# Second rotation buffers, a fourth score bank, a third bank for the up-projections, and two blocks of x scaled by ScalarE, in a hybrid encoder layer

## The reference, cut to what matters

```python
def hybrid_layer(x, mem, g_pre, w_in, w_conv, attn_sink, g_mem, w_mem_kv, w_up_a, w_up_b, w_up_m, w_out, g_post):
    h = rms_norm(x, g_pre)                       # x: 1024 tokens x 1024
    (a_b, a_c, a_x, a_z, b_q, b_k, b_v, b_z, m_q, m_z, gate_logits) = jnp.split(h @ w_in, idx, axis=-1)
    ya = short_gated_conv(a_b, a_c, a_x, w_conv) * silu(a_z)
    q, k = partial_rope(b_q, pos), partial_rope(b_k, pos)      # 8 query heads, 2 key heads, 64 wide
    yb = window_attention_with_sink(q, k, b_v, attn_sink) * silu(b_z)   # +-128 tokens
    mk, mv = split(rms_norm(mem, g_mem) @ w_mem_kv)            # 256 memory tokens
    ym = memory_cross_attention(m_q, mk, mv) * silu(m_z)
    gates = sigmoid(gate_logits)                               # 3 branches x 1024
    merged = gates[0] * (ya @ w_up_a) + gates[1] * (yb @ w_up_b) + gates[2] * (ym @ w_up_m)
    return x + rms_norm(merged @ w_out, g_post)
```

## Time and profile before

| | us |
|---|---|
| median of 3 runs | 968.27 |
| the three runs | 965.97 to 968.99 |
| the profiled execution | 967.6 |
| its span | 965.8 |

### The profile page before, as it was taken

One profiled execution on the slowest core, in us unless ns is written; L12 is line 12 of the kernel. 1 busy time (PEld: TensorE's weight loads), 2 busy tenths in 40 slices (PEclk: granted clock), 3 DMA queues, 4 the chain that ended last, 5 costly groups with the idle time before them and its releaser, 6 DMA issues. The chain is left out here.

```text
span 965.8 us, 12506 instructions
## 1 busy us (share of the span) xinstructions
PE 925.0 (96%) x4360; PEld 770.9 (80%) x4360; DVE 621.4 (64%) x1055; ACT 419.9 (43%) x800; POOL 386.9 (40%) x266
## 2 busy tenths in 40 slices
PE   5999779999999999999999999999998999999997
PEld 4787668888888888888888888888887788888885
DVE  5799856556565656655568178878896366664443
ACT  7322446444444456544461533333443534332211
POOL 2557834444333344443333844444442635210000
PEclk9999899999999999999999999999999899999999
DMA  7125545243424243434345512323222964542222
GB/s 278 66 75 137 137 134 166 99 145 106 148 99 145 99 134 98 163 104 149 105 141 160 157 55 77 87 85 90 87 68 80 319 227 148 200 169 68 88 88 87
DMA packets 79629, 122.33 MB, mean 127 GB/s; under 512 B 6992, under 2 KB 38864, under 8 KB 79568
## 3 DMA queue, kind: packets, MB, share of 16 engines
q1 hardware_dynamic: 79568, 121.55, 38.7%
HBM read 88.49 MB, written 33.03 MB: 126 GB/s over the span
## 5 line engine op out<-in xcount | busy, mean ns | idle before, releaser
L623 POOL TENSOR_TENSOR ring<-spots,ring 128x512 fp32r<-128x512 f32 x218 | 309.3, 1422 | 406.4 <-ACT ring L1020 394.2
L698 PE MATMUL pm<-hc,ring 128*128 128x512 f32 x728 | 287.9, 395 | 5.7 <-ACT ring L1020 5.5
L700 PE MATMUL pm<-hc,ring 128*128 128x512 f32 x728 | 284.5, 391 | 0.0
L699 PE MATMUL pm<-hc,ring 128*128 128x512 f32 x728 | 284.3, 391 | 0.0
L1020 ACT ACTIVATE ring<-spots 128x512 fp32r<-128x512 f32 x218 | 136.2, 628 | 258.9 <-PE pm L700 191.0
L698 PEld LDWEIGHTS pm<-hc,ring 128*128 128x128 f32 x728 | 137.3, 189 | 33.1 <-issue 6.5
L700 PEld LDWEIGHTS pm<-hc,ring 128*128 128x128 f32 x728 | 137.2, 188 | 29.4
L699 PEld LDWEIGHTS pm<-hc,ring 128*128 128x128 f32 x728 | 137.4, 189 | 26.8
L970 PE MATMUL pm<-hc,ring 128*128 128x512 f32 x192 | 76.1, 396 | 3.3 <-DVE area L1773 3.3
L971 PE MATMUL pm<-hc,ring 128*128 128x512 f32 x192 | 75.8, 395 | 0.0
L972 PE MATMUL pm<-hc,ring 128*128 128x512 f32 x192 | 75.7, 394 | 0.0
(11 more groups left out here) (198 smaller groups left out, 1518.2 us busy)
## 6 DMA issues: line engine op xcount, KB each, us to landing
spots<-in_w SPq DMA_DIRECT2D x116, 256.0 KB, 3.2
raw_d<-area SPq DMA_DIRECT2D x72, 256.0 KB, 2.0
area<-raw_d SPq DMA_DIRECT2D x24, 512.0 KB, 3.5
area<-in_x SPq DMA_DIRECT2D x16, 512.0 KB, 4.9
spots<-in_wup SPq DMA_DIRECT2D x24, 256.0 KB, 3.8
q_d<-area_r SPq DMA_DIRECT2D x16, 256.0 KB, 4.0
area_r<-q_d SPq DMA_DIRECT2D x8, 512.0 KB, 4.3
area<-raw_d SPq DMA_DIRECT2D x16, 256.0 KB, 3.6
```

The lines of the kernel that those rows point to most:

```text
L623: nc.gpsimd.tensor_tensor(ring[:, n % RING, 1, :], operand(n), ring[:, n % RING, 0, :].bitcast(F32), ALU.subtract).then_inc(lo_made, 1)
L698: pe.matmul(bank, hi, moving_hi(k), start=(k == 0), stop=False)
L699: pe.matmul(bank, hi, moving_lo(k), start=False, stop=False)
L700: mm = pe.matmul(bank, lo, moving_hi(k), start=False, stop=(k == HC - 1))
```

## The change

Four parts, and the order of the programs around them:

- **Blocks 6 and 7 of x** are scaled by ScalarE, after its root for them and VectorE's inverse. Product 5 of the first pair has no turns ahead of it, product 6 those of chunk 8, product 7 those of chunks 9 and 10, and from there it is as before.
- **Rotations** have two high buffers and two low ones (the low part overwrites the rotated tile). rope_high waits for no store; times_cos(j) waits for the stores of rotation j - 2. The rotations stand later in the order of each engine, between combinations, weight sums and weight splits; SyncE's stores stand behind more weight loads.
- **Scores**: the fourth head's scores go to pv and wait for the last output to have left it, no longer for the first mask.
- **Up-projections** rotate over three pairs of banks, and three of them run their first three chunks before the fourth. The first gate has the other gate buffer and is loaded at P4 of the last pair, once the last cross scores are done.

The diff, cut to what the prediction speaks of (left out: the same edits of names in the loads, the gate's drain and the semaphores' declarations):

```diff
@@ -89,7 +89,7 @@
 
 AREA = 14400
 X0, B11F, B21F, B12F, B22F, T3F = 0, 8192, 10240, 12288, 0, 2048
-COS0, SIN0, SWAP0, ROT1, QHI0, QLO0, ROT0, VR0, VP0 = 4096, 5120, 6144, 7168, 0, 1024, 2048, 3072, 12288
+COS0, SIN0, SWAP0, ROT1, QHI0, ROT0, VR0, VP0 = 4096, 5120, 6144, 7168, 0, 2048, 3072, 12288
 QS0, KWH0, KWL0, PR0, PTH0, PTL0, OS0, OO0 = 0, 1024, 1792, 2560, 4096, 5632, 7168, 7680
 O0 = 10240
 SIG0, SB0 = 8192, 9728
...
-        rope_hi_f32, rope_lo_f32 = rope_hi_r.bitcast(F32), rope_lo_r.bitcast(F32)
+        rope_high_at = [f32r(QHI0 + n * SEQ, SEQ) for n in range(2)]
+        rope_low_at = [f32r(at, SEQ) for at in (ROT1, ROT0)]
         memx = f32(MX0, 2 * D).rearrange("p (b d) -> p b d", b=2)
...
             return tile_banks[t % 3]
...
 
...
             return f32(Y0 + n % 4 * SEQ, SEQ)
+
+        def score_bank(h):
+            return pv[:, 0:WIN] if h == GROUP - 1 else sa[:, BANKS[h], 0:WIN]
+
+        def gate_of(g):
+            return gate[:, (g + 1) % 2, :]
 
         def bank_of(p, name):
...
+        inv_made, xs_act = sem("inv_made"), sem("xs_act")
...
+        def wait_stored(eng, j):
+            eng.wait_ge(rope_stored[j], 16 * (5 if ROPES[j][1] is None else 4))
...
             def store_rope(j):
                 c = ROPES[j][1]
+                high, low, done = rope_high_at[j % 2].bitcast(F32), rope_low_at[j % 2].bitcast(F32), rope_stored[j]
                 sp.wait_ge(rope_lo, j + 1)
...
                     if c is None:
-                        sp.dma_start(kh_d[own, g, :], rope_hi_f32[own, :]).then_inc(k_stored, 16)
-                        sp.dma_start(kh_d[other, g, :], rope_hi_f32[own, :]).then_inc(k_stored, 16)
+                        sp.dma_start(kh_d[own, g, :], high[own, :]).then_inc(done, 16)
+                        sp.dma_start(kh_d[other, g, :], high[own, :]).then_inc(done, 16)
...
@@ -412,14 +422,13 @@
             sp.dma_start(sinb, sin).then_inc(rope_landed, 16)
             for j in range(4):
                 load_spot(j, 2)
-            store_rope(0)
             load_spot(A11, 3)
             load_spot(A12, 3)
-            store_rope(1)
+            store_rope(0)
             load_spot(A21, 3)
             load_spot(A22, 3)
+            store_rope(1)
             store_rope(2)
-            store_rope(3)
...
                     store_raw(p, 0, 1, c12)
+
+            def load_gate(g):
+                if g == 0:
+                    sp.wait_ge(mscored, 2 * NB)
+                elif g == 1:
+                    sp.wait_ge(mpv_done, NB)
+                elif g - 2 < KC:
+                    sp.wait_ge(up_taken, g - 1)
+                else:
+                    sp.wait_ge(merged_done, g - 1 - KC)
+                sp.dma_start(gate_of(g), raw_d[GATE[g // KC] + g % KC - T_GA]).then_inc(gate_landed[g % 2], 16)
 
             for p, name in ORDER[N_DIRECT:]:
                 if p == "m":
...
                     load_spot(A12, p + 1)
                     load_spot(A21, p + 1)
+                    if p == P_DIRECT:
+                        store_rope(3)
                     store_block(p - 1, "next P2")
...
+                elif name == "P4" and p == P_LAST:
+                    load_gate(0)
                 store_block(p, name)
...
@@ -582,7 +597,6 @@
                 nh, k = divmod(n, KC)
                 sp.dma_start(spots[:, 4 + n % 3, :], wout[nh][:, k * HALF:(k + 1) * HALF]).then_inc(wo_landed[n % 3], 16)
 
-            load_gate(0)
             load_gate(1)
...
             def rope_low(j):
                 pool.wait_ge(rope_hi, j + 1)
-                nc.gpsimd.tensor_tensor(rope_lo_r, rotated(j), rope_hi_f32, ALU.subtract).then_inc(rope_lo, 1)
+                nc.gpsimd.tensor_tensor(rope_low_at[j % 2], rotated(j), rope_high_at[j % 2].bitcast(F32),
+                                        ALU.subtract).then_inc(rope_lo, 1)
...
             low_part(8)
             for j in (0, 2):
                 low_of_combination(T2, j)
+            low_part(9)
             rope_low(0)
-            low_part(9)
+            low_part(10)
             rope_low(1)
-            low_part(10)
+            low_part(11)
             for j in (0, 2):
                 low_of_combination(T4, j)
-            low_part(11)
             low_part(12)
+            low_part(13)
             rope_low(2)
-            low_part(13)
-            rope_low(3)
             low_part(14)
             for j in (0, 2):
                 low_of_combination(T1, j)
             low_part(15)
+            rope_low(3)
             low_part(16)
             rope_low(4)
...
@@ -717,9 +732,10 @@
 
                 for n in range(2 * KC):
                     half, kk = divmod(n, KC)
-                    if 1 <= n and n + 3 < 2 * KC:
-                        pe.wait_ge(h_copied, n)
-                        turn_x(n + 3)
+                    for m in {5: (), 6: (8,), 7: (9, 10)}.get(n, (n + 3,)):
+                        if 4 <= m < 2 * KC:
+                            pe.wait_ge(h_copied, m - 3)
+                            turn_x(m)
...
@@ -770,7 +786,10 @@
                 half, k = divmod(n, KC)
                 for b in [2 * pair + b for pair in pairs for b in range(2)]:
                     if half and b % 2 == 0:
-                        pe.wait_ge(xs_made, 3 + b // 2)
+                        if b:
+                            pe.wait_ge(xs_act, 1)
+                        else:
+                            pe.wait_ge(xs_made, 3)
                     at = X0 + (4 * half + b) * D + k * P
                     mm = pe.transpose(spare[n % 4][:, b * P:(b + 1) * P], area[:, at:at + P], ident[:, :])
...
                     pe.wait_ge(kl_landed, 32 * (i + 1))
                 for h in range(GROUP):
-                    b = BANKS[h % 3]
                     if h == 3:
-                        pe.wait_ge(masked, GROUP * gr + 1)
+                        at_least(pe, o_taken, gr)
                     elif gr == 0:
                         pe.wait_ge(v_made, 2)
                         pe.wait_ge(cos_made, len(ROPES))
                     else:
                         pe.wait_ge(pt_lo_made, 3 * (gr - 1) + h + 1)
-                    pe.matmul(sa[:, b, 0:WIN], q_stack[:, g, h, :], kwin_hi[:, g, :], start=True, stop=False)
-                    pe.matmul(sa[:, b, 0:WIN], q_stack[:, g, h, :], kwin_lo[:, g, :],
+                    pe.matmul(score_bank(h), q_stack[:, g, h, :], kwin_hi[:, g, :], start=True, stop=False)
+                    pe.matmul(score_bank(h), q_stack[:, g, h, :], kwin_lo[:, g, :],
                               start=False, stop=True).then_inc(scored, 1)
...
             def up(g, chunks, half_major, begin, end):
-                n, br, bank = NS + g, g // KC, g % 2
+                n, br, bank = NS + g, g // KC, tile_bank(g)
                 r, y = (NS + g) % RING, y_of[g // KC]
                 pe.wait_ge(hi_made, n + 1)
                 pe.wait_ge(lo_made, n + 1)
                 if begin:
-                    if g >= 2:
-                        pe.wait_ge(up_taken, g - 1)
+                    if g >= 3:
+                        pe.wait_ge(up_taken, g - 2)
                     elif g == 0:
                         pe.wait_ge(d_made, PAIRS - P_DIRECT)
                         pe.wait_ge(c12, PAIRS - P_DIRECT)
+                    elif g == 2:
+                        pe.wait_ge(mpt_act, NB)
+                        pe.wait_ge(mpt_dve, NB)
                     else:
                         pe.wait_ge(c_made, PAIRS - P_DIRECT)
                         pe.wait_ge(c21, PAIRS - P_DIRECT)
...
-                    if g < 2:
+                    if g < 3:
...
-                    dst = pm[:, bank, cols]
+                    dst = bank[:, cols]
...
             cross_values(NB - 1)
-            for g in range(2):
+            for g in range(3):
                 up(g, YA_ORDER[:3], False, True, False)
-            for g in range(2):
+            for g in range(3):
                 up(g, YA_ORDER[3:], False, False, True).then_inc(slot_done, 1)
-            for g in range(2, UPS):
+            for g in range(3, UPS):
                 up(g, (0, 1, 2, 3), True, True, True).then_inc(slot_done, 1)
...
                 if b < 2:
-                    pe.wait_ge(up_taken, UPS - (0 if p else 1))
+                    pe.wait_ge(up_taken, UPS - 2 + p)
...
             def take_a(p):
                 wait_slot(act, p, "P1")
                 at_least(act, c12, p - P_DIRECT - 1)
-                if p == P_DIRECT:
-                    act.wait_ge(rope_lo, 2)
                 nc.scalar.copy(sum_of(p), bank_of(p, "P1")).then_inc(a_made, 1)
...
                 if n == 6:
                     roots(3)
+                    act.wait_ge(inv_made, 1)
+                    for b in range(6, NB):
+                        ins = nc.scalar.activation(f32(X0 + b * D, D), f32(X0 + b * D, D), ACT.Copy,
+                                                   scale=st[:, 9, b:b + 1])
+                    ins.then_inc(xs_act, 1)
...
@@ -1083,10 +1107,7 @@
```

(60 more changed lines are left out.)

36 lines of the change are left out of this document (13 added, 23 removed).

## The result

The changed kernel takes **952.07 us** in the median (951.25 to 952.89, 4 runs), against 968.18 of the kernel before beside it (965.97 to 968.99, 4 runs). The ratio is **0.984, 95% interval 0.982 to 0.986**: 16.1 us less. The profiled execution took 951.5 with a span of 949.7, 16.1 less than the span before. The forecast was 950.7, from 943.5 to 957.

The account below looks back on a forecast made before the run. TensorE was taken to bound the kernel, so only its idle or slow time could go. 0.7 + 3.5 + 7.0 + 6.4 = 17.6 us off 967.6 gave 950.0, plus 0.7 for the median: 950.7 us, range 943.5 to 957.

Parts of the forecast that it names:

- Start: Scaling of blocks 6 and 7 of x: product 5 no longer waits behind the transposes, gaining 0.7 us.
- Rotation stage: Rotations up to the first scores: second buffers and new order bring c12 earlier, gaining 3.5 us, bounds -2 to 8.9.
- The alternation: Rotation stage: VectorE and GpSimd exclude each other and take turns, so the last rotation ends at 106.2, against 109.45 before.
- Score banks: Attention score groups: the gap ahead of the 7th score matmul goes in 15 of 16 groups, 0.47 each, 7.0 us.
- the 2.3 us of cover: Score groups: the previous output leaves pv by 319.13, the 7th matmul comes at 321.4, so the new wait costs nothing.
- Up-projections: Up-projections: the first gate's stall and the slow clock behind it go; the fourth projection starts 6.4 us earlier.
- the 2.9 for the clock: Up-projections: 14 matmuls after the restart take 6.03 us instead of 3.17; this 2.9 joins the 3.5 us stall.
- B: Rotation stage: GpSimd's operations fall under VectorE's PSUM reads and idle time, all 8.9 us come, 945.3 us; chance 0.15.
- C: Rotation stage gives nothing or loses 2 us, as later cos(2) holds tile 5 or a store binds, 954.2 to 956.2; chance 0.15.
- D: Up-projections: gate 1 or the y loads take the late gate's place, half of 6.4 us gone, 953.9 us; chance 0.07.
- E: Score groups: the fourth head waits for the output's drain in each group, kernel slower, 971.2 us; chance 0.03.
- F: Whole kernel: each removed stall reappears at the next dependency, no gain, within 0.3%, 968 us; chance 0.03.

Follow-up runs that it names:

- The nine executions above: Profiled runs of several kernels, six with the old rotations and three with the new: first shuffle to first score takes 84.97 us and 81.53 us in the mean.
- the cut low parts: The changed kernel with GpSimd's low parts of the five rotations cut to 64 of 1024 columns: 945.6 us, ratio 0.9771.
- the keys early: The changed kernel with the clearing of the key windows moved to after c22, ahead of c12: 949.59 us, ratio 0.9811.

## Why the prediction was right

- **Start, 0.7 us.** The steps came as worked out. ScalarE's pair took 2.19 (put at 2.1) and began 0.4 later than put, so the transposes waited until 29.50 instead of 28.95. Product 4 came 0.48 later in this profile than in the one of before, so the marker shows 0.2; measured from product 4 it is 0.7. Over all traces it is 0.75; alone it measured 0.5 with 0.9 either way. Chunk 7's multiplication did not hold product 7.
- **Rotation stage, 3.5 us.** This was the term with the widest bounds (-2 to 8.9). The alternation, laid out operation by operation, met the trace: tile 5 at 81.74 (82.0), rotate(4) ending 106.27 (106.2), P5 at 111.18 (111.2), c12 at 118.54 (117.6 to 118.3). The layout left the start's gain out; rotate(0), from whose end it counts, ended 0.2 earlier in this trace (62.05), so the 43.95 us to the end of rotate(4) were 44.22. What it laid on P5 was right, too: the wait of 3.1 (2.89) and the slow restart, which made c12 wait 0.56. Beyond c12 there was one step with no size: it took the key load to be as long as before. It took 6.7 from issue to first score instead of 5.8, which is why the profile shows 2.5 and not 3.5. The nine executions above show that this is more the luck of the profile of before than a loss: the means of the stretch are 3.4 apart, and alone the part measured 2.9 with 1.2 either way.
- **Score banks, 7.0 us.** 6.9 by the markers, 6.7 over all traces, 7.0 alone. The gap of the earlier trace rows times 15 is the gain, and the 2.3 us of cover ahead of the new wait for the output sufficed: it appears nowhere.
- **Up-projections, 6.4 us.** 6.4 by the markers, but 5.25 over all traces, and 5.9 alone. The stall and the slow restart behind it both went. The term was read off one profile, and that one had the longest slow restart of the four: the 2.9 for the clock is about 1 us too large for the other three. That the markers of the same profile give 6.4 again is luck of the same reading and does not confirm it. What the prediction did not see is that it counted one cure twice: the third bank alone brings all 6.4. It named the early gate as what makes gate 0 ready in time; with three banks a gate as late as before is early enough. The sum doesn't change by that.
- **The rivals.** B (the rotations go faster by all 8.9) falls with the measured 2.9 of that part alone, and the cut low parts show what it would have needed: GpSimd out of VectorE's way. C (no gain there) falls with the same number; one half of its condition, tile 5 held by a later cos(2), did occur and was in the forecast's sum. D, E and F did not occur: no wait for gate 1, none for the output in pv, and of the removed stalls only the rotation stage's came back, in part.
- The sum was 17.6, the measured change 16.1 by the medians and by the spans, 13.9 to 17.6 by the interval. By the two single profiles, 1.0 of the 1.5 between would be in the rotation stage and 0.5 at the start. Over all traces those two terms are right to 0.1, and 1.1 of the 1.5 is in the up-projections.

## What to carry to other kernels

Where two engines exclude each other, lay out their queues one operation after the other before pricing a removed wait: here that turned 8.9 us of stalls into 3.5, and it was within half a microsecond over 45 us of work. A wait in the trace is worth only what it keeps from the next wait's end: the 2.9 us ahead of P5 were worth nothing that could be measured; a memset moved ahead in the queue of the engine that ends the last wait brought the scores 1.1 us forward, and the medians 1.6. A term read off a single profile carries that execution's luck: take the same stretch from several. And before two cures are applied to one stall, price each alone; one spare pair of banks did here what an earlier load was added for.

## What the runs showed of the hardware

- The clock may fall behind a wait, not only in it, and the same wait need not bring it down. Behind the 2.89 us wait ahead of P5 the changed kernel's first two matmuls took 0.47 and 0.42, and the third, 0.53 us after the restart, 0.62, at 1.2 GHz (0.67 granted from 110 to 115; 0.66 when the same kernel was run again). In the kernel with the keys early, which is the same up to that point, the wait is 2.89 as well, and TensorE stays at 2.4 GHz (1.00 granted in that stretch):

```profile
110.91 0.47 PE L713 MATMUL pm<-hc,ring 128*128 128x512 f32 x1 [2.89 <-POOL ring L637]
...
111.45 0.39 PE L715 MATMUL pm<-hc,ring 128*128 128x512 f32 x1
```

  After the 1.59 us wait at tile 5 nothing slowed. After the 5.5 us wait of the kernel before the first matmul was slow at once (0.76).
- How long the clock stays down behind the same wait differs between executions too: 0.83 granted from 105 to 110 in the kernel before, 0.53 with the score banks alone, and 13 matmuls at the lower level behind the first gate's wait against 7 or 8. The key load took 5.8 to 7.3 us from its issue to the first score over all kernels here. Between the kernel before and the score banks alone it differed by 1.2 us, the start by 0.45 and the stretch with the slow clock by 0.3: the first score moved by 1.9 us between kernels with the same rotation stage, more than the smallest term of the sum.
